# Low halves on VectorE, outputs parked as split halves, scores between the two heads' transposes, and a token-major last product

## What is computed

```python
o_a = from_heads(forgetting_attention(to_heads(qa, H_FOX), ...))      # 8 heads, causal, with a decay
o_b = from_heads(chunk_band_attention(to_heads(qc, H_CHK), ...))      # 8 heads, 640 keys per 128 queries
g_a, g_b = jnp.split(jax.nn.sigmoid(gates), N_BRANCH, axis=-1)        # gates = a part of h @ w_in
merged = g_a * (o_a @ w_branch_a[l]) + g_b * (o_b @ w_branch_b[l])
x = x + merged @ w_out[l]
h2 = rms_norm_2(x, norm2[l])
x = x + jnp.square(jax.nn.relu(h2 @ w_up[l])) @ w_down[l]
return rms_norm_2(x, final_norm)
```

## Time and profile before

| | us |
|---|---|
| median of three runs | 3613.49 |
| lowest and highest | 3606.68, 3614.68 |
| profiled execution | 3608.5 |
| its span | 3606.8 |
| mean granted TensorE clock, share of full | 0.943 |

### The profile page before, as it was taken

How to read it: one execution, slowest core, us unless ns; L and a number is a source line. 1 busy time by engine, 2 the same in 40 slices (tenths; PEclk the granted TensorE clock), 3 DMA queues, 4 the chain that set the end, 5 groups by cost and what they waited for, 6 DMA issues and landing times.

```text
span 3606.8 us, 49466 instructions
## 1 busy us (share of the span) xinstructions
PE 3196.2 (89%) x20350; PEld 2561.3 (71%) x20350; DVE 1629.3 (45%) x1893; ACT 967.3 (27%) x1407; POOL 721.5 (20%) x310
## 2 busy tenths in 40 slices
PE   7997888566979999999875999999989999999997
PEld 5885777455758878878744886666668777777776
DVE  4522555276164444444470114445444544444444
ACT  2102344355232212212231113333343211111112
POOL 1221211100142212212132341000022222222210
PEclk9998899787989999999987999999989999999998
DMA  4222000121131111111035353234434411111111
GB/s 153 93 100 94 21 22 21 31 59 41 30 130 57 47 41 52 47 41 52 18 112 121 116 187 105 82 106 131 123 121 144 159 47 47 47 47 47 47 35 47
DMA packets 227140, 272.20 MB, mean 75 GB/s; under 512 B 8873, under 2 KB 181042, under 8 KB 227002
## 3 DMA queue, kind: packets, MB, share of 16 engines
q1 hardware_dynamic: 212026, 219.36, 20.6%
q10 hardware_dynamic: 14976, 50.86, 3.5%
HBM read 199.38 MB, written 70.81 MB: 75 GB/s over the span
## 4 chain that ended last, share of the span: by engine, by line
PE 77%; DVE 9%; issue 8%; ACT 3%; another core or an unknown queue 1%; POOL 1%; DMA 1%; SPq 0%; DVEq 0%; ACTq 0%; POOLq 0%
PE ps L350 57%; PE ps L1601 5%; PE ps L474 4%; PE ps L1652 2%; PE ps L1673 2%; PE ps L1631 1%; PE ps L1176 1%; DVE cb L2103 1%; PE ps L1203 1%; DVE y L2013 1%; PE ps L1633 1%; DVE xl L392 1%; DVE pbuf L1843 1%; POOL src L1966 1%
## 5 line engine op out<-in xcount | busy, mean ns | idle before, releaser
L350 PE MATMUL ps<-xh,wh 128*128 128x512 f32 x2416 | 754.5, 394 | 48.1 <-POOL wl L327 44.7
L350 PE MATMUL ps<-xl,wh 128*128 128x512 f32 x2416 | 747.5, 391 | 0.0
L350 PE MATMUL ps<-xh,wl 128*128 128x512 f32 x2416 | 745.4, 390 | 0.0
L327 POOL TENSOR_TENSOR wl<-wraw,wh 128x1024 fp32r<-128x1024 f32 x167 | 404.7, 2424 | 1580.4 <-ACT wh L322 1580.4
L350 PEld LDWEIGHTS ps<-xh,wh 128*128 128x128 f32 x2416 | 454.9, 189 | 155.0 <-issue 53.1
L350 PEld LDWEIGHTS ps<-xl,wh 128*128 128x128 f32 x2416 | 455.8, 189 | 95.4
L350 PEld LDWEIGHTS ps<-xh,wl 128*128 128x128 f32 x2416 | 455.3, 188 | 95.3
L322 ACT ACTIVATE wh<-wraw 128x1024 fp32r<-128x1024 f32 x167 | 177.0, 1061 | 1135.9 <-PE ps L350 1039.9
L2013 DVE TENSOR_TENSOR y<-ps,y 128x1024 f32<-128x1024 f32 x216 | 262.1, 1223 | 266.2 <-PE ps L350 266.2
L350 PE MATMUL ps<-fh,dh 128*128 128x512 f32 x864 | 275.0, 400 | 51.5 <-DVE y L2013 35.8
L350 PE MATMUL ps<-fl,dh 128*128 128x512 f32 x864 | 271.9, 396 | 0.0
(11 more groups left out here) (294 smaller groups left out, 3895.8 us busy)
## 6 DMA issues: line engine op xcount, KB each, us to landing
wraw<-in_w_up SPq DMA_DIRECT2D x76, 512.0 KB, 3.9
wraw<-in_w_in SPq DMA_DIRECT2D x67, 512.0 KB, 3.9
draw<-in_w_down SPq DMA_DIRECT2D x27, 1024.0 KB, 4.9
proj<-stage ACTq DMA_DIRECT2D x34, 512.0 KB, 2.6
residual<-src ACTq DMA_DIRECT2D x32, 512.0 KB, 4.9
hres<-residual SPq DMA_DIRECT2D x24, 512.0 KB, 4.8
wraw<-in_w_out SPq DMA_DIRECT2D x16, 512.0 KB, 4.3
qk_hi<-hs ACTq DMA_DIRECT2D x16, 512.0 KB, 2.7
```

The source lines that it names most:

```text
L327: nc.gpsimd.tensor_tensor(wl[:, s, :, :], wraw[:, s, :, :], wh[:, s, :, :].bitcast(F32), ALU.subtract).then_inc(w_lo, 1)
L350: mm = nc.tensor.matmul(ps[:, bank + h, :], w, x[:, h * HALF:(h + 1) * HALF], start=start and k == 0, stop=stop and k == 2)
```

## The change

Five things are changed.

1. **Gate weights' low halves**: DVE makes them (`gate_lo`, L1835), in the block's step after the one in which a unit ended, behind the scales and ahead of the maxima. POOL's 16 are gone. `gate_evac` of a unit that ends at head 0's groups goes ahead of the maxima, and there is one stage buffer.
2. **Parked outputs** are stored as two halves. DVE makes the low one (`low`, L1828) for every pair, at n = 5 and at n = 0 of the next pair; ACT issues two stores per half and waits for the low one; SP loads both straight to `xh` and `xl`. ACT's seven copies and POOL's seven subtractions are gone.
3. **Scores** of n+2 are set between the transposes of head 0 and of head 1 of block n (ahead of both before), and inside, the high products of head 0 come first.
4. **The fill table** gives pair 1 48 matmuls more and pair 6 48 fewer (none in its blocks 5 to 7). Turned groups rotate over three banks from there on.
5. **The second feed-forward stage** becomes token-major in its down product (`token_products`: `fh`, `fl` loaded, `dh`, `dl` moving, 96 matmuls as before). `y` is turned to token-major at the start: 64 transposes inside the second and third up unit (`turn_residual`), copies by ACT, and the residual comes through two buffers `rt`. The tail is per token tile: add, ACT's square with its row sum and root, DVE's reciprocal and one operation for both factors, with the gain as a broadcast row, and SP's store.

```diff
-        FILL = [[[1, 1], [1, 1], *TWO[2:]], TWO, THREE, THREE, TWO, TWO, TWO, None]
+        ONE = [*TWO[:5], [0, 0, 0, 0], [0, 0, 0, 0], [0, 0, 0, 0]]
+        NONE = [[0, 0]] * 4 + [[0, 0, 0, 0]] * 4
+        FILL = [[[1, 1], [1, 1], *TWO[2:]], THREE, THREE, THREE, TWO, TWO, ONE, NONE]
...
-                    diagonal = b < FOX_PAIRS and hi == size
+                parts = [(lo // HALF, slice(first + lo, first + min(size, lo + HALF))) for lo in range(0, size, HALF)]
+                for m in range(2):
+                    for c, k in parts:
+                        mm(ps[:, 2 * m + c, 0:k.stop - k.start], qs2[:, m, q], kh2[:, m, k], start=True, stop=False)
+                for c, k in parts:
                     for m in range(2):
-                        mm(ps[:, 2 * m + lo // HALF, 0:hi - lo], qs2[:, m, q], kh2[:, m, k], start=True, stop=False)
+                        ins = mm(ps[:, 2 * m + c, 0:k.stop - k.start], qs2[ROWS[m], m, q], kl2[ROWS[m], k],
...
-                    a2_act.wait(pe, f"ot{b - 1}1", 0)
-                elif pair == 2 and b == PAIRS - 1:
+                    a2_dve.wait(pe, f"xl{b - 1}1", 0)
+                elif pair == 2:
                     a2_dve.wait(pe, f"xl{b}0", 0)
...
-                        scores(b, n + 2)
                     k = 0
                     for m in range(2):
+                        if m and n + 2 < TT:
+                            scores(b, n + 2)
                         for g in groups_of(b, n):
                             turn(b, n, m, g)
-                            if FILL[b] is not None:
-                                fill(FILL[b][n][k])
+                            fill(FILL[b][n][k])
...
-                act.wait_ge(park_loaded[t], 16)
-                nc.scalar.activation(xh[:, t, :], xl[:, t, :].bitcast(F32), ACT.Copy).then_inc(park_hi, 1)
+                act.dma_start(parked[b, 0][:, part], ost[:, h, :].bitcast(F32)).then_inc(parked_stored[h], 16)
+                a2_dve.wait(act, f"xl{b}{h}", 0)
+                act.dma_start(parked[b, 1][:, part], ost_lo[:, h, :].bitcast(F32)).then_inc(parked_stored[h], 16)
...
                 n = U_GATES + u
                 dve.wait_ge(mm_done, n + 1)
-                stage_free(dve, QKV2 + u)
-                nc.vector.tensor_tensor(stage[:, u % 2, :], bank2(3), rstd[:, :], ALU.mult).then_inc(evac_done, 1)
+                dve.wait_ge(stage_stored[0], STAGES1 + 16 * (4 + u))
...
                 a2_act.wait(dve, f"ot{b}{h}", 0)
-                part = slice(h * HALF, (h + 1) * HALF)
-                a2_dve.done(nc.vector.tensor_tensor(xl[:, b, part], ps[:, 5, :], xh[:, b, part].bitcast(F32),
-                                                    ALU.subtract), f"xl{b}{h}")
+                if b < PAIRS - 1:
+                    dve.wait_ge(parked_stored[h], 32 * b)
+                    lo, hi = ost_lo[:, h, :], ost[:, h, :]
+                else:
+                    part = slice(h * HALF, (h + 1) * HALF)
+                    lo, hi = xl[:, b, part], xh[:, b, part]
+                a2_dve.done(nc.vector.tensor_tensor(lo, ps[:, 5, :], hi.bitcast(F32), ALU.subtract), f"xl{b}{h}")
...
+            def gate_lo(u):
+
+                n = U_GATES + u + 2
+                dve.wait_ge(w_hi, n + 1)
+                dve.wait_ge(w_lo, n)
+                nc.vector.tensor_tensor(wl[:, n % 2, :, :], wraw[:, n % 2, :, :], wh[:, n % 2, :, :].bitcast(F32),
+                                        ALU.subtract).then_inc(w_lo, 1)
...
+                    for u in UNIT_ENDS.get((b, n, 0), ()):
+                        gate_evac(u)
+                    for u in lows:
+                        gate_lo(u)
+                    lows = []
+                    if n == 0 and b:
+                        low(b - 1, 1)
+                    if n == 5:
+                        low(b, 0)
                     if n + 2 < TT:
                         maxima(b, n + 2)
-                    for u in UNIT_ENDS.get((b, n, 0), ()):
-                        gate_evac(u)
-                    if b == PAIRS - 1 and n == 5:
-                        low(b, 0)
                     for g in groups_of(b, n):
                         turned_copy(dve, a2_dve, b, n, 1, g)
                     for u in UNIT_ENDS.get((b, n, 1), ()):
                         gate_evac(u)
+                    lows += [u for part in range(2) for u in UNIT_ENDS.get((b, n, part), ())]
                     if n == TT - 1 and b + 1 < PAIRS:
...
                 for h in range(2):
-                    sp.wait_ge(parked_stored[h], 16 * (t + 1))
-                sp.dma_start(xl[:, t, :].bitcast(F32), parked[t]).then_inc(park_loaded[t], 16)
+                    sp.wait_ge(parked_stored[h], 32 * (t + 1))
+                sp.dma_start(xh[:, t, :].bitcast(F32), parked[t, 0]).then_inc(park_loaded[t], 16)
+                sp.dma_start(xl[:, t, :].bitcast(F32), parked[t, 1]).then_inc(park_loaded[t], 16)
...
+        def token_products(pe, steps, c, d, par):
+
+            pe.wait_ge(d_lo, d + 2)
+            steps.wait(pe, "l1", c)
+            for m in range(TT):
+
+                if m != 1:
+                    pe.wait_ge(down_added, KT * d + max(m - 1, 0) + 1)
+                t = slice(m * P, (m + 1) * P)
+                for kt in range(2):
+                    mm = three_products(4 + 2 * (m % 2), fh[:, par, kt, t], fl[:, par, kt, t], dh[:, kt, :],
+                                        dl[:, kt, :], kt == 0, kt == 1)
+                mm.then_inc(down_done, 1)
...
+        def turn_residual(pe, kt):
+
+            s = kt % 2
+            pe.wait_ge(rt_loaded[s], 16 * (kt // 2 + 1))
+            if kt == 1:
+                pe.wait_ge(stat_root, 6)
+            elif kt:
+                pe.wait_ge(y_turned, kt - 1)
+            for t in range(TT):
+                mm = nc.tensor.transpose(ps[:, 4 + 2 * s + t // 4, t % 4 * P:t % 4 * P + P],
+                                         rt[:, s, t * P:(t + 1) * P], ident[:, :])
+            mm.then_inc(rt_turned, 1)
...
+        def turned_residual_act(act, kt):
+
+            act.wait_ge(rt_turned, kt + 1)
+            nc.scalar.activation(y[:, :, kt * P:(kt + 1) * P].rearrange("p (a t) c -> p a t c", a=2),
+                                 bank2(2 + kt % 2).rearrange("p a (t c) -> p a t c", t=4), ACT.Copy)\
+                .then_inc(y_turned, 1)
...
+            for m in range(TT + 1):
+                if m < TT:
+                    dve.wait_ge(down_done, KT * d + m + 2)
+                    nc.vector.tensor_tensor(y[:, m, :], bank2(2 + m % 2), y[:, m, :], ALU.add).then_inc(down_added, 1)
+                if m:
+                    t = m - 1
+                    dve.wait_ge(out_root, m)
+                    nc.vector.reciprocal(token_rstd[:, t:t + 1], token_ss[:, t:t + 1]).then_inc(out_rstd, 1)
+                    dve.wait_ge(out_rstd, m)
+                    nc.vector.scalar_tensor_tensor(out=y[:, t, :], in0=y[:, t, :], scalar=token_rstd[:, t:t + 1],
+                                                   in1=gain_row[:, :], op0=ALU.mult, op1=ALU.mult)\
+                        .then_inc(out_ready, 1)
...
+            for m in range(TT):
+                act.wait_ge(down_added, KT * d + m + 2)
+                nc.scalar.activation(token_sq[:, :], y[:, m, :], ACT.Square, accum_out=token_ss[:, m:m + 1])\
+                    .then_inc(out_sum, 1)
+                act.wait_ge(out_sum, m + 1)
+                nc.scalar.activation(token_ss[:, m:m + 1], token_ss[:, m:m + 1], ACT.Sqrt, bias=small[:, 0:1],
+                                     scale=1.0 / D).then_inc(out_root, 1)
...
+            sp.wait_ge(x_lo, 32)
+            sp.wait_ge(x_sq, 48)
+            for kt in range(2):
+                sp.dma_start(rt[:, kt, :], residual[kt]).then_inc(rt_loaded[kt], 16)
+            load_down(sp, 0, DOWN1, a["w_down_2"])
+            for k in range(2):
...
+            for kt in range(2, KT):
+                sp.wait_ge(rt_turned, kt - 1)
+                sp.dma_start(rt[:, kt % 2, :], residual[kt]).then_inc(rt_loaded[kt % 2], 16)
...
+            for t in range(TT):
+                sp.wait_ge(out_ready, t + 1)
+                sp.dma_start(out[t * P:(t + 1) * P, :], y[:, t, :]).then_inc(out_stored, 16)
...
-            for n in range(U_GATES + 2, U_BRANCH + 2):
-                split_lo(pool, n, n % 2)
-            for t in range(PAIRS - 1):
-                pool.wait_ge(park_hi, t + 1)
-                nc.gpsimd.tensor_tensor(xl[:, t, :], xl[:, t, :].bitcast(F32), xh[:, t, :].bitcast(F32),
-                                        ALU.subtract).then_inc(park_lo, 1)
...
-            for t in range(TT):
-                s = t % 2
-                act.wait_ge(out_turned, t + 1)
-                if t >= 2:
-                    act.wait_ge(out_stored[s], 16 * (t // 2))
-                nc.scalar.activation(out_tile[:, s, :], bank2(s), ACT.Copy, scale=token_rstd[:, t:t + 1])\
-                    .then_inc(out_ready, 1)
-                act.wait_ge(out_ready, t + 1)
```

(28 more changed lines are left out.)

141 lines of the change are left out of this document (70 added, 71 removed).

## The result

The changed kernel takes 3624.7 us (median of 6 runs, 3618.3 to 3633.1) against 3609.1 for the kernel before (6 runs, 3605.7 to 3614.7). The ratio is 1.0044, with a 95% interval of 1.0028 to 1.0061: slower by 0.44%. The forecast was 3631, slower; the range 3570 to 3652 holds the time. The forecast rise over the profiled execution of before was 22.7 us; the medians rise by 15.6.

A forecast was written before the change was run, and what follows sets the result against it. TensorE, busy for 89% of the span, was taken as the bound, so changes count by its idle time. 3608.5 − 24.2 (tail) + 3 (feed-forward start) + 43.9 (scores' place) = 3631 us; range 3570 to 3652.

The forecast's parts named there:

- The tail, minus 24: From TensorE's last matmul to the end of the span: 32.05 us become 7.8, a gain of 24.2 us.
- The start, plus 3: Start of the feed-forward stage: 64 transposes 4.4, copy wait 1.1, filled gap minus 2.55; 3 us, bounds 0 and +7.
- +7 for the start: Start of the feed-forward stage: upper bound of 7 us if transposes don't keep the clock up.
- The scores' new place, plus 44: Second attention: TensorE idles before the next transposes, waiting for VectorE; 43.9 us over eight pairs, bounds +20 and +65.
- the chain: VectorE after a block's scores: maxima, copy of head 1's turned group, reciprocal, first scale; 2.95 us before the next transposes.
- the lock's gap: TensorE's 2.45 us wait, once in each of pairs 0 to 6, when GpSimd's low half slows VectorE's scales; gone with the change.
- as frequent as today: Attention: the low clock was taken as unchanged, since gaps of 1.75 and 2.3 us replace one of 2.45.
- The first (the chain is covered, 3561): First rival, attention: wait ahead of each block's transposes at most 0.3 us, VectorE mostly ahead; 3561 us, chance 0.17.
- the clock's 12 us: Term of the first rival, attention: half of the low clock's price goes, minus 12 us.
- The gaps' 19.4 less 5: Term of the first rival, attention: 19.4 us of transposes' waits for scales go, 5 us of gaps remain.
- The clock rival (3653): Third rival: clock falls more often, in pairs 6 and 7 without gate matmuls and behind new waits; +22 us, chance 0.10.

The follow-up runs named there:

- The alone run: The kernel before with only the token-major last product, turned residual and new tail, nothing changed in the attention: 3589.8 us, ratio 0.9939.

## Why the prediction was right, and where it was not

**The tail, minus 24**: 32.05 became 7.3 us, minus 24.7. The terms were 1.23, 1.06, 0.19, 0.27, 0.2, 1.45; measured 1.22, 1.06, 0.19, 0.29, 0.16, 1.28. **The start, plus 3**: 2.8 us in the profile. The alone run has both at −22.2. The sum of the start was right by luck. It took the 1.09 us of the earlier trace rows for eight transposes at the low clock and halved it, 4.4 us for all. Those eight ran at the full clock, as the kernel before shows by stretch (they lie in the second):

```profile
3587.29:3592.90 5.61, 5.61 (x27) 5.61 (x28) 0.00 (x0) 2.23 (x2) 0.00 (x0) 0.50 0.23 93
3593.00:3603.00 10.00, 5.10 (x39) 3.91 (x37) 0.00 (x0) 6.02 (x6) 0.00 (x0) 1.00 0.66 266
```

So 64 cost 6.6 us and not 4.4, and the wait that is gone ahead of the second down product and the low clock that is gone, neither of them in the sum, made up for it.

The rule that transposes don't keep the clock up (the Trainium skill, TensorE: Matmul & The Clock Gate, "Part 4: PE-mode transpose") gave +7 for the start. In this trace the stretch with the 64 transposes, between the matmuls of two units, has a granted clock of 1.00, so it did not bite here. The two rows above go further: from 3587.29 to 3592.9 us TensorE did nothing but transposes, busy all the time, and the granted clock then rose from 0.50 to 1.00. Here the trace and the page differ.

**The scores' new place, plus 44**: 41.1 us in the profile (480.0 to 521.1), 37.5 by the medians, and by pairs, predicted and measured: pair 0 10 and 10.5; pair 1 14.5 and 12.2; pair 2 2.5 and 1.8; pair 3 2.5 and 0.5; pairs 4 and 5 7.2 and 6.5, 5.4; pair 6 −3 and +3.2; pair 7 +3 and +0.9. The mechanism holds: undoing it gives 51.5 us back, and cutting the chain at VectorE gives back 46. The idle time alone was put too high in the pairs with four gate matmuls per block: 12.4 us forecast, 9.8 and 10.2 in pairs 4 and 5. It was put too low in pair 6, where 18.4 us stand in place of some 14 (5.2 + 12 − 3).

But the term was named for one edit and held the net of several. Three of its parts were mis-sized:

- The order inside the scores was not priced at all and gains 10 us (12.5 by TensorE's busy time).
- The low halves on VectorE were priced at nothing net, with the lock's gap gone and another in its stead. They gain 13 us (6.6 to 17.7 in the four pairs of runs).
- The low clock "as frequent as today" was wrong. The granted clock went from 0.95 and 0.73 to 0.92 and 0.73 by stretch, and with the scores first to 0.96 and 1.00: by the estimate of the prediction 67, 100 and 34 us at the lower level. In the changed kernel the place takes 61.3 us of the stage in the two profiles (521.1 and 459.8), and only 41.7 of them are idle time: for the same instructions TensorE is busy for 432.3 us with the new place and 412.7 with the old.

The first two hide part of what the place costs, the third adds to it, and they nearly cancel. So the 44 was right as a net figure, partly by luck, and the place alone on the kernel before (75 us against 25 to 50) shows what was missed.

**Parked outputs, nothing**: right in sum where the scores come first (3582.8 against 3577 to 3583), though two parts cancel there. With the new place 21 us of a comparison remain for them and the evacuations' place, which the prediction did not price.

**The fill table**: counted as neutral in its matmuls and mildly bad in pair 6. Mild as forecast: 8 us with the scores first, none to be told with the new place.

**The rivals.** The first (the chain is covered, 3561) was wrong in its condition. Its price was too low as well: with the chain out of the way the kernels take 3573 and 3579 us, and both have the inner order's 10 us, which it did not count; without that it is 3583.6. Of its terms the clock's 12 us is about right (434.3 less 412.7 less 12.5 leaves 9 us of busy time). The gaps' 19.4 less 5 is not: the stage idles as long as before, 47.2 us, since other waits came in. It also said by which rule the change ought to win (the Trainium skill, SBUF — State Buffer, "Who interferes with whom"). The lock's absence did gain 13 us; it is the same change's other part that lost more. The clock rival (3653) came about half true in the changed kernel: 100 us at the lower level where it had twice 67, and TensorE busy for 10 us more than the inner order alone would leave (432.3 against 434.3 less 12.5). In the kernel with the place alone it came nearly in full, 124 us and 18.6.

**What would show it**: the idle time of seven pairs went from 36.3 to 75.2 us (forecast 75), the transposes wait for the scales at the block shown for 1.51 us, the tail is under 8 us, GpSimd is silent, the forty widest banded scales take 550 ns in the mean. That the transposes wait 1 to 2 us in nearly every block did not come: 33 waits of 1 us or more in 64 blocks. The group of the transposes waits 63.7 us in all, well over the 30 that would have contradicted me; of the low clock, 0.92, the same holds.

A version with the low halves, the parked halves, the inner order and the token-major part, but the scores first and the old fill table, takes 3565.1 us and beats both kernels. It also has the evacuations' new place, which was never undone by itself; the 2.3 us waits in pairs 2 and 3 say that it is worth a try.

## What to carry to other kernels

Where an engine works through a fixed row and another answers it, ask at each item what stands between it and its predecessor on the answering engine, and how long the first engine's own row covers that. Moving a long item from ahead of a pair of short ones to between them halves that cover without changing a single cost. When several edits come together, price each at the place it leaves and the place it goes to, and check by undoing one at a time: here one line's order was worth 51.5 us out of a change that showed 15.6. An item that waits for another engine, such as the evacuation of a unit, holds up everything queued behind it even if that is ready: look at what stands behind it, not only at its cost.

## What the runs showed of the hardware

- Eight matmuls, four of 128 rows and four of 64, take 1.71 us in four alternating groups and 1.32 us in two. Over the stage that is 12.5 us of TensorE's busy time. Which property of the order costs this is not shown.
- Added idle time came with a lower granted clock. Where the place alone added 57 us of idle time, TensorE was busy for another 18.6 us with the same instructions, and the granted clock of pair 7 was 0.60 (0.73 before). In the changed kernel pair 7 has 0.73, and 1.00 with the scores first.
- Transposes alone brought the clock up: in the tail of the kernel before, TensorE did nothing else from 3587.29 us on, and the granted clock went from 0.50 to 1.00 at 3592.9 us. It stayed there to 3603 us, with transposes alone and TensorE busy for 5.10 of 10 us.
- Where GpSimd subtracts while VectorE scales, two scales of 640 columns take 3.01 us instead of 1.02, and forty of them 700 ns in the mean instead of 550.
